# A dense Trainium2 kernel: the first projections of two feed-forward networks as seven half-size products per pair of tiles

## The reference, cut to what matters

```python
def _swiglu(h, w_gu, w_down):                 # w_gu (1024, 2*2816), w_down (2816, 1024)
    gate, up = jnp.split(h @ w_gu, 2, axis=-1)
    return (jax.nn.silu(gate) * up) @ w_down

x = x + 0.5 * _swiglu(_rmsnorm(x, ffn1_norm), ffn1_w_gu, ffn1_w_down)
h = _rmsnorm(x, mix_norm)                     # projections, Hyena and RWKV branches
...
x = x + merged @ w_out
x = x + 0.5 * _swiglu(_rmsnorm(x, ffn2_norm), ffn2_w_gu, ffn2_w_down)
x = _rmsnorm(x, final_norm)
```

## Time and profile before

| | |
|---|---|
| runs shown | 2938.39, 2945.51, 2954.10 us; median 2945.51 |
| profiled execution, span from first to last instruction | 2946.3 us |
| PE busy | 2793.7 us |
| DVE busy | 1522.3 us |
| ACT busy | 870.5 us |
| POOL busy | 355.7 us |
| mean granted PE clock, share of full speed | 0.977 |

### The profile page before, as it was taken

The page is one execution under the profiler, slowest core; times in us unless marked ns, Lnnn a source line. Parts: engine busy times, 40 slices in busy tenths (PEclk is TensorE's granted clock), DMA queues, the critical chain, the costliest instruction groups (busy, mean ns, idle before and its releaser), DMA issues. The chain is left out here.

```text
span 2946.3 us, 41141 instructions
## 1 busy us (share of the span) xinstructions
PE 2793.7 (95%) x17739; PEld 2226.3 (76%) x17739; DVE 1522.3 (52%) x2124; ACT 870.5 (30%) x1164; POOL 355.7 (12%) x334
## 2 busy tenths in 40 slices
PE   8999999888889999999999999899999899999998
PEld 6888877577766678788888785678888665688887
DVE  5555454666676743465554524363364655462343
ACT  3222133311135222322222435332222434432222
POOL 1111010211010000021110002121020100120110
PEclk9999999999999999999999999899999999999999
DMA  5555542000030112355554220223343210222331
GB/s 151 170 155 169 167 129 66 2 3 3 3 113 11 43 50 93 100 164 161 170 163 157 86 72 30 72 72 108 94 149 123 53 46 16 72 91 95 100 100 57
DMA packets 264325, 271.28 MB, mean 92 GB/s; under 512 B 9631, under 2 KB 245126, under 8 KB 263951
## 3 DMA queue, kind: packets, MB, share of 16 engines
q1 hardware_dynamic: 248784, 206.78, 22.9%
q0 software_dynamic: 15360, 61.87, 6.3%
HBM read 266.53 MB, written 2.10 MB: 91 GB/s over the span
## 5 line engine op out<-in xcount | busy, mean ns | idle before, releaser
L920 DVE TENSOR_TENSOR mix_wl<-ring_raw,mix_wh 128x2048 fp32r<-128x2048 f32 (+2 forms) x66 | 153.1, 2319 | 221.4 <-ACT mix_wh L807 221.3
L707 PE MATMUL mix_ps<-h_mix_hi,mix_wh 128*128 128x512 f32 x624 | 244.2, 391 | 0.0
L709 PE MATMUL mix_ps<-h_mix_lo,mix_wh 128*128 128x512 f32 x624 | 242.8, 389 | 0.0
L807 ACT ACTIVATE mix_wh<-ring_raw 128x2048 fp32r<-128x2048 f32 (+2 forms) x66 | 117.6, 1782 | 212.6 <-PE mix_ps L713 162.1
L707 PE MATMUL ffn_ps<-h_rw_hi,ffn_wh 128*128 128x512 f32 x448 | 175.3, 391 | 0.0
L709 PE MATMUL ffn_ps<-h_rw_lo,ffn_wh 128*128 128x512 f32 x448 | 174.3, 389 | 0.0
L920 DVE TENSOR_TENSOR mlp_wl<-ring_raw,mlp_wh 128x2048 fp32r<-128x2048 f32 (+1 forms) x38 | 96.7, 2545 | 131.1 <-ACT mlp_wh L807 131.1
L920 DVE TENSOR_TENSOR mlp_wl<-mlp_raw,mlp_wh 128x2048 fp32r<-128x2048 f32 x36 | 93.2, 2589 | 133.2 <-ACT mlp_wh L807 133.2
L713 PE MATMUL mix_ps<-h_mix_hi,mix_wl 128*128 128x512 f32 x624 | 154.2, 389 | 0.0
L707 PE MATMUL mlp_ps<-view,mlp_wh 128*128 128x512 f32 x384 | 149.7, 390 | 0.0
L709 PE MATMUL mlp_ps<-view,mlp_wh 128*128 128x512 f32 x384 | 149.4, 389 | 0.0
(11 more groups left out here) (607 smaller groups left out, 6122.6 us busy)
## 6 DMA issues: line engine op xcount, KB each, us to landing
ring_raw<-in_mlp_w SPq DMA_DIRECT2D x32, 1024.0 KB, 5.4
mlp_raw<-in_mlp_w SPq DMA_DIRECT2D x32, 1024.0 KB, 5.4
ffn_sraw<-in_ada_w POOLq DMA_DIRECT2D x34, 768.0 KB, 5.2
ffn_raw<-in_ffn_w_gu SPq DMA_DIRECT2D x44, 512.0 KB, 5.2
ring_raw<-in_ffn_w_gu SPq DMA_DIRECT2D x44, 512.0 KB, 4.6
mix_sraw<-in_ada_w POOLq DMA_DIRECT2D x22, 768.0 KB, 5.2
ring_raw<-in_w_in SPq DMA_DIRECT2D x14, 1024.0 KB, 5.4
ring_raw<-in_a_w_in SPq DMA_DIRECT2D x12, 1024.0 KB, 5.3
```

Of the source, the lines that this page charges most:

```text
L707: nc.tensor.matmul(ps[:, it.banks[t], :], w(h, k, t), xh[:, k, :], start=it.first and k == it.k0, stop=False)
L709: nc.tensor.matmul(ps[:, it.banks[t], :], w(h, k, t), xl[:, k, :], start=False, stop=False)
L807: nc.scalar.activation(slot(wh, it), slot(raw, it), ACT.Copy).then_inc(hi_ready, 1)
L920: nc.vector.tensor_tensor(slot(wl, it), slot(raw, it), slot(wh, it).bitcast(F32), ALU.subtract)\
```

## The change

The first projection's pair (weights A, two tiles of 128 output features by 8 k-tiles; input B, 8 k-tiles by 512 tokens) is seen as a product of 2 x 2 blocks: two output tiles, two halves of k, two halves of the tokens. It is computed in Strassen's form (Winograd's variant) with seven products of 4 k-tiles by 256 tokens instead of eight. Per pair that takes four sums of weight blocks (POOL, 128 x 512 elements each), and per network four sums of input blocks (DVE, 128 x 1024 each, `form_lowers`; cut into parts by ACT and DVE). The products accumulate in PSUM where they can; three intermediate values are copied out (ACT, `snap`) and three sums are formed by DVE (`seven_adds`). The gate product then goes over two halves (`gate_out`), ACT makes its high part in an operation of its own (`ff_uppers`) and POOL the low one.

The high and low parts of weights now lie in rings of eight slots of 4 k-tiles by 128; a pair of the new form uses seven, an item of the old form four. Parts are made by the slot, each one as soon as the product that used the slot is done (`it.makes`).

Each network goes in two halves of 11 pairs: first projection, second projection over these 11 k-tiles (items of 5 and 6 k-tiles, 8 items), then the same again. The first two pairs of a network stay in the old form.

The side product moves: none in a network's first half of the first projection; 8 halves in each second projection's part, 8 in the second half of the first projection (pairs 1 to 8, its steps spread over the pair), 8 in the recurrent branch's input projection, and 4 each in the five Gemms from the Hyena gate to the output projection. The first MLP has none. `dense` asks for room for 56 semaphores instead of 40.

```diff
 def lay_out(steps, ahead=0):
+    it.seven = st.seven if gi >= st.plain else None
+    if it.seven:
+        it.s, it.f0 = sevens.up() - 1, products.n
+        products.up(7)
+        left = 7 * (len(st.groups) - gi)
+        if gi == st.plain:
+            place_at += -(place_at + left) % (SLOTS // 2)
+        it.slots = [(place_at + i) % SLOTS for i in range(7)]
...
 def dense(nc, e, tag, steps, buf, guest=None, ahead=None):
-        sb, pb, sem = opened(nc, s, tag, 40)
+        sb, pb, sem = opened(nc, s, tag, 56)
...
                 if it.n >= 2:
-                    sp.wait_ge(lo_ready, it.n - 1)
+                    was = items[it.n - 2]
+                    if was.seven:
+                        sp.wait_ge(part_lo, was.f0 + 7)
+                    else:
+                        sp.wait_ge(lo_ready, was.c)
...
+            def seven_products(it):
+                plan = [(P_A11, corner(it), of_x(0, low_half), None), (P_S1, beside_corner(it, 1), of_form(Seven.T1), 1),
+                        (P_S2, corner(it), of_form(Seven.T2), 2), (P_S4, beside_corner(it, 1), of_x(ks, high_half), None),
+                        (P_S3, corner(it), of_form(Seven.T3), 3), (P_A12, beside_corner(it, 0), of_x(ks, low_half), None),
+                        (P_A22, corner(it), of_form(Seven.T4), 4)]
+                for i, to, x, form in plan:
...
+                    elif i == P_S2:
+                        pe.wait_ge(snapped, 3 * it.s + 1)
+                    elif i == P_S4:
+                        pe.wait_ge(snapped, 3 * it.s + 2)
+                    elif i == P_S3:
+                        pe.wait_ge(snapped, 3 * it.s + 3)
+                    elif i == P_A12:
+                        pe.wait_ge(added, 3 * it.s + 1)
+                    elif i == P_A22:
+                        pe.wait_ge(added, 3 * it.s + 2)
+                    pe.wait_ge(part_hi, it.f0 + i + 1)
...
+                    for k in range(ks):
+                        nc.tensor.matmul(to, h[:, k, :], x(xh, k), start=begins and k == 0, stop=False,
+                                         skip_group_check=not begins)
+                        nc.tensor.matmul(to, h[:, k, :], x(xl, k), start=False, stop=False, skip_group_check=not begins)
+                    pe.wait_ge(part_lo, it.f0 + i + 1)
...
         @block.scalar
+            def seven_steps(it):
+                for i in range(7):
+                    if i < 3:
+                        act.wait_ge(product_done, it.f0 + i + 1)
+                        if it.s > 0:
+                            act.wait_ge(added, 3 * it.s - (0, 1, 2)[i])
+                        nc.scalar.activation(snap(it, i), beside_corner(it, 1) if i == 1 else corner(it), ACT.Copy)\
+                            .then_inc(snapped, 1)
+                    if i == 2 and last_seven(it):
+                        ff_uppers(last_seven(it))
+                    if i == 6 and it.pair:
+                        act.wait_ge(added, 3 * it.s + 3)
+                        gate = f[:, it.use[0] % 2, :]
+                        nc.scalar.activation(gate, gate, ACT.Silu).then_inc(f1_ready, 1)
+                    uppers(it.makes[i], (it, i))
...
         @block.vector
+            def seven_steps(it, half, made):
+                for i in range(7):
+                    if i == 0 and last_seven(it):
+                        gate_out(last_seven(it))
+                    seven_adds(it, i)
+                    lowers(made)
+                    made = it.makes[i]
+                    if half is not None and i in SIDE_STEPS:
+                        side_part(it.gemm, half, SIDE_STEPS.index(i))
...
         @block.gpsimd
+            def weight_sums(it):
+                wait_loaded(pool, it)
+                was = items[it.n - 1] if items[it.n - 1].seven else None
+                earlier = lambda i: pool.wait_ge(part_lo, was.f0 + i + 1) if was else None
+                a11, a12, a21, a22 = (quarter(it, j, k) for j in range(2) for k in range(2))
+                s = lambda n: weight_sum(it, n)
+                earlier(P_S1)
+                nc.gpsimd.tensor_tensor(s(S1), a21, a22, ALU.add).then_inc(sum_ready, 1)
...
                     for i, it in enumerate(st.items):
...
+                        if st.seven and i > 0:
+                            ff_lowers(st.items[i - 1])
+                        if it.n + 2 < len(items) and items[it.n + 2].seven:
+                            weight_sums(items[it.n + 2])
...
+        def feed_forward(h, tag, first, sides):
+            gu, w_down, steps = I[f"{tag}_w_gu"], I[f"{tag}_w_down"], [first]
+            seven = sevens(e, 2 * n_ff, floats(e, 38, 4), floats(e, 42, 2))
+            for half in range(2):
+                up = Gemm(gu, DT, h, 2 * n_ff, "swiglu", dst=ff, parts=None if half else first, at=half * n_ff, seven=seven,
+                          plain=0 if half else 2, side=sides[2 * half], side_from=1)
+                seven.made_by = seven.made_by or up
+                down = Gemm(w_down[half * n_ff * P:(half + 1) * n_ff * P, :], n_ff, ff, DT, "add", dst=x, factor=0.5,
+                            parts=up, side=sides[2 * half + 1])
+                steps += [up, down]
+            return steps, down
...
-            steps, down = feed_forward(h, "ffn1", first, (ada(0, 0, 33), ada(0, 30, 18)))
+            steps, down = feed_forward(h, "ffn1", first, (None, ada(0, 0, 12), ada(0, 12, 12), ada(0, 24, 12)))
...
+            hy_out = Gemm(I["hy_out"], HT, zh, DT, "gate", dst=merged, gate=sig, parts=cut_z, side=kvada(6, 6))
...
+            rw_out = Gemm(I["rw_out"], RT, zr, DT, "merge", dst=merged, gate=sig, parts=cut_y, side=ada(1, 0, 6))
...
-            mlp, last = mlp_steps(e, I, 0, y, h, ml_out, [ada(1, 32 + 8 * i, 8, 2 * P) for i in range(2)])
+            mlp, last = mlp_steps(e, I, 0, y, h, ml_out)
```

More of the change, by code:

```diff
@@ L397, in __init__, with side_items @@
         self.feeds, self.of_tile, self.padded = None, {}, padded
+        self.at, self.seven, self.plain, self.side_from = at, seven, plain, side_from
+    def side_items(self):
+        n = 2 * -(-self.side[0].shape[-1] // self.side[1])
+        return self.items[self.side_from:self.side_from + n]
 class Norm:
@@ L441, in lay_out @@
     taps, saves, halves, sides, columns = (Count() for _ in range(5))
-    groups, factors = 0, 0
+    plain, sevens, products, ff, f1 = (Count() for _ in range(5))
+    groups, factors, place_at, at_slot, need = 0, 0, 0, {}, None
     user, of_use, loads, items = {}, {}, [0, 0], []
@@ L476, in lay_out @@
                     [act_out.up() if st.kind in ("copy", "tokens") else dve_out.up() for _ in js]
+                if it.seven:
+                    it.made = it.out[:len(it.use)]
+                    it.out = it.out[-1:] * 2
+                    it.ff = [ff.up() for _ in it.use]
+                it.f1 = [f1.up() for _ in it.use] if pair or not it.seven else []
                 it.slot_free = [of_use.get(u - 2) for u in it.use]
@@ L778, in _ @@
                             sum_tile(fed, j)
-                    if st.side:
+                    if st.side and st.side_from + st.side_n == len(st.items):
                         owed = st
@@ new lines, in uppers, with ff_uppers @@
+            def uppers(units, need):
+                for it, i in units:
+                    if i is None:
+                        upper(it)
+                    else:
+                        upper_part(it, i, need)
+            def ff_uppers(it):
+                for t, u in enumerate(it.use):
+                    act.wait_ge(dve_out, it.made[t])
+                    nc.scalar.activation(it.gemm.dst[0][:, it.js[t], :], f[:, 2 + u % 2, :], ACT.Copy).then_inc(ff_hi, 1)
+            def seven_steps(it):
[13 more added lines that the diff above has]
+                    uppers(it.makes[i], (it, i))
+                if it is it.gemm.items[-1]:
+                    ff_uppers(it)
@@ L809, in square, with form_uppers @@
+            def form_uppers(st):
+                for n, order in ((Seven.T1, 1), (Seven.T2, 3), (Seven.T3, 2), (Seven.T4, 4)):
+                    act.wait_ge(formed, st.form_at + order)
+                    nc.scalar.activation(st.seven.hi[:, n, :, :], form_of(st, n), ACT.Copy).then_inc(form_hi, 1)
             def square(st, k):
@@ new lines, in gate_out @@
+            def gate_out(it):
+                st, c = it.gemm, it.seven.snaps[:, 3, :]
+                if it.pair:
+                    u = it.use[0]
+                    dve.wait_ge(f1_ready, it.f1[0])
+                    dve.wait_ge(product_done, it.f0 + 7)
+                    if u > 2:
+                        dve.wait_ge(low, u - 2)
+                    gate, out = f[:, u % 2, :], f[:, 2 + u % 2, :]
+                    nc.vector.tensor_tensor(out[:, 0:LQ], gate[:, 0:LQ], corner(it), ALU.mult)
+                    nc.vector.tensor_tensor(out[:, LQ:L], gate[:, LQ:L], c, ALU.mult).then_inc(dve_out, 1)
@@ L1060, in _ @@
                             owed = None
```

(5 more changed lines are left out.)

346 lines of the change are left out of this document (263 added, 83 removed).

## The result

The changed kernel takes **3080.06 us** (median of 4 runs, 3078.7 to 3082.6), the kernel before 2946.02 in the same comparison (4 runs, 2938.4 to 2954.1): ratio **1.0459**, 95% interval 1.0433 to 1.0485. Slower by 134 us, where the prediction said 3075 (+130) with a range of 2965 to 3130. The profiled execution's span is 3078.4 us, 132.1 longer than before.

The account below looks back on a forecast made before the run. PE sets the time in the kernel before; seven-product pairs would run at DVE's pace, slowed by POOL. Terms 34 + 20 + 30 + 22 + 20 + 4 = +130 on 2946.3, 1 taken off: 3075 us, range 2965 to 3130.

Parts of the forecast that it names:

- PE's part: Seven-product pairs: 84 matmuls at 0.118 us, 9.9 us a pair against 10.9; PE alone would gain 39 us in all.
- Pairs and starts: First projections of both networks: pairs at DVE's pace +34, starts of first halves +20, of second halves +30 us.
- Starts: Beginnings of the halves: PE waits for DVE's first sum, +10 us a network in first halves, +15 in second.
- Side product's cycle at the norms: Second projections: single buffer turns in 8.95 us against 7.5 an item, so the norm comes 11 us later, twice: +22.
- Between the branches: Hyena gate to output projection: side halves on all 20 items delay DVE's cut of the merged rows: +20 us (12 to 24).
- Rest: Side halves behind the recurrent input projection +4 and the output projection +2, first MLP losing its sixteen -2: +4 us.
- Signs: Seven-product pairs: PE waits before the sixth product, POOL sums over 1.28 us, lower parts over 0.68; pairs 13 to 14 and 11.
- All low ends: Whole kernel with every term at its low end: 3020 us stated.
- rival (3): 256-column matmul bound by its weight load: 0.145 us, 12.2 a pair, some 25 us on top, 3100; forecast with it 0.62.
- rival 2: Only one mechanism holds, DVE and POOL colliding (2990) or the side chain (2987); chance 0.18.
- Rival (1): PE sets the pace; POOL's sums fall where DVE waits and the side chain is absorbed: 2917 us, faster; chance 0.12.

Follow-up runs that it names:

- old_pairs: Changed kernel with all pairs back in the old form (48 matmuls of 512 columns), halves and new side places kept: 2987.8 us.
- one_load: Changed kernel with the side product loaded once instead of eight times in the two second halves, DVE's steps all kept: 3043 us.
- split_load: Changed kernel with each side half loaded in two DMAs, the first sent after side step 2 of 4: 3030 us.
- split_sums: Changed kernel with side loads in two parts, sent ahead in all stages, and the four weight sums made by DVE instead of POOL: 2977 us.
- split_all: Changed kernel with side loads in two parts, sent ahead in all stages, weight sums still on POOL: 29 us slower than split_load.
- best_of_old: Changed kernel with side loads ahead, side halves moved off the short items between the branches, all pairs in the old form: 2967.6 us, ratio 1.0039.

## Why the prediction was right

Right in sign and size, 3075 for 3080, and by its two mechanisms, DVE and POOL in each other's way and the single side buffer. The terms were less good than their sum: 84 predicted and 85.6 measured for pairs and starts, 22 and 9.9 at the norms, 20 and 25.8 between the branches, 4 and 3.8 for the rest, and 7.0 in the heads stage, for which nothing was predicted. That the total is 2 us off (+132 for +130) is luck, as these errors cancel. Measured on the traces:

- **PE's part** (84 matmuls at 0.118): 0.120 us, 10.1 a pair, 0.8 less than the old form's 10.9. Right, and the rival of a matmul bound by its weight load (0.145) is out. So is the estimate from the Trainium skill, "TensorE: Matmul & The Clock Gate", section "Back-to-back issue gap", of 109 ns, as it was for 512 columns. The section gives that formula for an isolated matmul; its figure for a stream of matmuls of 512 columns, 131 ns, is further still from the 227 ns of the earlier trace rows.
- **Pairs and starts** (34 + 20 + 30 = 84): the first projections take 42.0 and 43.6 us more than before, 85.6. But before has 22 side halves in each of them and the changed kernel 8, and I had left their matmuls out on both sides. Against old_pairs, where they lie alike, it is 4.9 and 5.9 in the first halves, 40.5 and 40.5 in the second, 91.8. Within it, pairs with side work took 15.4 us, not 13.5, pairs without 10.1 to 10.7, not 11.1. **The step that failed** in this term is that the side product's cycle was costed in the second projections and between the branches, and left out of the pairs. There a load has only the time from the seventh product of a pair to the third of the next, and it takes longer: 6.9 to 8.6 us from issue to landing in eight of the nine of that stage, where it is 4.9 to 5.1 in the second projection behind it. one_load without it gave 13.7: the predicted 13.5 was near the price of the collision alone. In the pairs without side work the collision is there in full (lower parts 1.17 us on average in the first half, 0.73 with the sums on DVE) but DVE's 9.5 us a pair stay under PE's 10.1, and it cost 0.5 us a pair (10.7, and 10.2 with the sums on DVE); I had put DVE at 10.4 at least, as if all five POOL operations met a lower part.
- **Starts**: DVE's first sum came at 71.2 in the first half (74 predicted) and 13.2 us behind the boundary of the second (20.6): the 6.3 us by which DVE was to be late there were not there. It was +9 and +10, for 10 and 15.
- **Side product's cycle at the norms** (+22): the second projections and norms take 3.6 and 6.3 us more than before, 9.9 together, and 7.9 of it in old_pairs too, so it isn't the seven products. It is the load: from the norm's own matmuls behind the last item to the next projection PE takes 9.0 and 22.8 us in the changed kernel, 6.1 and 16.8 with the load in two parts (split_load), 6.0 and 16.7 before. The end of the first network in the changed kernel, POOL and then DVE:

```profile
441.31 0.75 POOL L1411 DMA_DIRECT2D ffn_sraw<-in_ada_w  x1 [7.87 <-DVE ffn_acc L1266]
448.96 0.75 POOL L1411 DMA_DIRECT2D ffn_sraw<-in_ada_w  x1 [6.90 <-DVE ffn_acc L1266]
```

```profile
446.28 0.42 DVE L1263 TENSOR_SCALAR ffn_acc<-ffn_sraw,cond 128x384 f32<-128x384 f32 x1 [1.18 <-DMA ffn_sraw<-in_ada_w]
...
450.43 0.69 DVE L1228 SCALAR_TENSOR_TENSOR resid<-ffn_ps,resid 128x512 f32<-128x512 f32 x1 [1.16 <-PE ffn_ps L884]
...
454.05 2.58 DVE L1266 SCALAR_TENSOR_TENSOR ffn_acc<-ffn_sraw,cond,ffn_acc 128x384 f32<-128x384 f32 x4 [2.93 <-DMA ffn_sraw<-in_ada_w]
456.54 0.95 DVE L1302 RECIPROCAL ffn_sd<-ffn_sd 128x128 f32<-128x128 f32 x1
```

  A turn takes 7.65 us (441.31 to 448.96), not 8.95, just the 7.5 of an item, so DVE never falls back. The load lands after 5.0 us. The 6.2 of the earlier trace rows was the slowest of twelve loads of that stage of before; the other eleven took 5.0 to 5.5. Multiplied by eight halves, one slow row made 11 us. The reciprocal starts 6.1 us behind the last eviction, against 4.0 in the earlier trace rows.
- **Between the branches** (+20): +25.8. Size nearly right, place half right: PE does wait 6.0 us for the cut's lower part at the output projection (18 predicted), but the larger part stands earlier, 8.0 us ahead of the side product's own small matmuls on the short items, 5.4 for those matmuls (9 groups of 0.6, which the prediction left out "on both sides", though they move into a stage that had none) and the clock after the waits (0.95, 0.98 before).
- **Rest** (+4): +7.8 -2.8 -1.2. The wait behind the last item of the recurrent branch's input projection is 5.3 us, for 4 predicted.
- +7 of the difference is the heads stage, whose code the change doesn't touch and whose length varies by more than that from kernel to kernel.
- **Signs.** PE did wait for DVE ahead of the sixth product, and POOL's sums took over 1.28 us in the first half (1.38 to 1.63 on average) and lower parts up to 1.99. The pairs came out at 15.4 and 10.7, where I had put 13 to 14 and 11.
- **Sums on record.** All low ends together give 3027, not 3020, and rival (3) costs 14 x 1.1 + 8 x 2.3 = 34 us, not 25. Neither carries the forecast.

The errors of +22 at the norms and of the pairs' cycle had the same root, the load's time, in opposite directions. With one mechanism taken away (rival 2) the time fell to 3030 or 3047 and not to 2990, since the starts and the side work on the short items are there in either. Rival (1), PE sets the pace, nearly holds where DVE has no side work.

## What to carry to other kernels

Where no engine is full and PE still waits, look for a chain with one buffer, write down its turn (issue to landing, consumer's first to last step, next issue) and set it against the time of one item in every stage in which it will run; take the landing time from many rows, not one. When two prices fall into the same gap, removing either can show less than half (14 to 21 us of 43 to 46 in a network here): remove both before saying what a change is worth. And price the freed columns against the engine that makes the new operands: here 0.8 us of PE a pair (10.9 to 10.1) cost DVE 5.0 (8.7 us a pair with the sums on DVE, 52.39 of 60.40 us, against 2.28 for the lower part and 2 x 0.69 in the old form), and with everything mended nothing was left.

## What was not expected

- **A stage that no kernel touches varies by 31 us.** The heads stage in three kernels; PEclk is the number after the last bracket:

```profile
1768.60:2050.00 281.40, 264.68 (x1255) 198.21 (x1254) 131.21 (x198) 111.31 (x205) 52.06 (x55) 0.97 0.19 61
```

```profile
1825.70:2130.60 304.90, 290.90 (x1256) 213.98 (x1254) 131.45 (x198) 111.86 (x205) 52.19 (x55) 0.87 0.18 56
```

```profile
1738.60:2051.30 312.70, 298.70 (x1256) 217.89 (x1255) 131.46 (x198) 111.86 (x205) 52.16 (x55) 0.85 0.17 55
```

  These are split_sums, split_all and best_of_old. Same instructions, the same busy time on DVE, ACT and POOL, and the granted clock at 0.97, 0.87 and 0.85. Over 25 runs the kernel before took 2941 to 2976 us, with a mean clock of 0.981 to 0.966, a spread of the same size; no trace shows whether that lies in this stage too. What sets the clock there stays open.
- **A lower part beside a POOL operation has few durations.** Of the changed kernel's 280, 161 took under 0.75 us, 43 took 1.35 to 1.55, 57 took 1.65 to 1.85, one 1.99, and 18 lay in between. The Trainium skill, "SBUF — State Buffer", section "SBUF: two separate sides", says that whoever starts first holds the pair of ports for its whole instruction. By that, an estimate: an operation met at its start takes up to 0.68 + 1.28 = 1.96 us; the usual long one here is 1.78 and one took 1.99, so the trace agrees in kind.
- **The side load takes 7 us beside the pairs and mostly 5 elsewhere**, at a DMA share of 0.40 in the pairs and 0.49 between the branches: the share alone doesn't tell it. In two parts, each took 3.6 to 5.9 us beside the pairs (split_sums, first network).
